# Triangular inverses of a two-block model: the joining level in 32x32 blocks, transposes on VectorE, and attention and gating taken one turn later

## What is computed

```python
lhs = eye + jnp.einsum("nbhik,nbhjk->nbhij", kb, k) * decay * (1.0 - eye)
u = solve(lhs, v * beta[..., None])
w = solve(lhs, kb * jnp.exp(gc)[..., None])
attn = jnp.einsum("nbhik,nbhjk->nbhij", q, k) * decay
...
def step(state, inp):
    v_new = u_c - jnp.einsum("bhck,bhkv->bhcv", w_c, state)
    o = jnp.einsum("bhck,bhkv->bhcv", q_c, state) + jnp.einsum("bhij,bhjv->bhiv", attn_c, v_new)
    state = state * gl[..., None, None] + jnp.einsum("bhck,bhcv->bhkv", k_c, v_new)
...
o = _rms(o) * norm_w.astype(F32) * jax.nn.silu(z...)
```

## Time and profile before

| what | value |
|---|---|
| median of 3 runs | 2035.76 us |
| lowest and highest | 2029.8 and 2036.88 us |
| the profiled execution, its own time | 2028.58 us |
| its span in the profile | 2026.8 us |
| mean granted clock of TensorE over the span, of full speed | 0.951 |
| PE / DVE / ACT / POOL busy | 1742.4 / 907.8 / 631.6 / 127.7 us |
| turns of the first loop, start to start | 128.0, 126.7 and 128.7 us |
| turns of the delta rule, start to start | 92.9 us for one, 90.9 to 91.0 us for six |

### The profile page before, as it was taken

How to read it: one execution, slowest core, us unless ns; L and a number is a source line. 1 busy time by engine, 2 the same in 40 slices (tenths; PEclk the granted TensorE clock), 3 DMA queues, 4 the chain that set the end, 5 groups by cost and what they waited for, 6 DMA issues and landing times.

```text
span 2026.8 us, 38852 instructions
## 1 busy us (share of the span) xinstructions
PE 1742.4 (86%) x16211; PEld 1135.6 (56%) x16211; DVE 907.8 (45%) x1907; ACT 631.6 (31%) x1208; POOL 127.7 (6%) x247
## 2 busy tenths in 40 slices
PE   0799999999988889999999999999699647777777
PEld 0447466574663457768686777768544523333333
DVE  5223061340621355868677686868402531111162
ACT  1133152431520153545445363545200101111112
POOL 8201000010000000000000000000000010000020
PEclk9999999999977999999999999999899669999989
DMA  8211030110821221111112111111040069999851
GB/s 321 65 43 45 0 86 2 42 45 0 305 90 52 70 66 43 43 43 44 44 42 84 44 43 43 43 43 44 15 166 11 32 253 413 407 417 397 360 176 42
DMA packets 122364, 229.15 MB, mean 113 GB/s; under 512 B 9294, under 2 KB 92587, under 8 KB 109931
## 3 DMA queue, kind: packets, MB, share of 16 engines
q1 hardware_dynamic: 100480, 194.40, 26.6%
q10 hardware_dynamic: 17996, 24.24, 3.3%
q0 software_dynamic: 3744, 8.40, 1.2%
HBM read 203.81 MB, written 28.44 MB: 115 GB/s over the span
## 4 chain that ended last, share of the span: by engine, by line
PE 45%; DVE 11%; DMA 10%; issue 1%; ACT 1%; SPq 0%; DVEq 0%; POOL 0%; ACTq 0%; POOLq 0%
PE ps L1315 11%; DMA W<-in_moe_w_up_dram 9%; PE ps L2209 6%; PE ps L1326 4%; PE ps L2517 4%; PE ps L1085 3%; PE ps L1471 3%; PE ps L2675 2%; PE ps L1449 2%; DVE W L1966 2%; PE ps L1354 1%; PE ps L1364 1%; PE ps L1374 1%; DVE W L1971 1%; DVE arena L1849 1%
## 5 line engine op out<-in xcount | busy, mean ns | idle before, releaser
L1315 PE MATMUL ps<-hT,W 128*128 128x512 f32 x512 | 230.2, 594 | 1.4 <-ACT hT L1109 1.0
L2517 PE MATMUL ps<-W,yT 128*32 128x256 f32 x2048 | 125.4, 400 | 45.4 <-DMA W<-in_moe_w_up_dram 33.9
L1315 PEld LDWEIGHTS ps<-hT,W 128*128 128x128 f32 x512 | 94.9, 190 | 98.2 <-issue 96.4
L539 PE MATMUL ps<-hT,W 128*128 128x512 f32 x288 | 137.9, 612 | 0.0
L2517 PEld LDWEIGHTS ps<-W,yT 128*32 128x32 f32 x2048 | 69.3, 115 | 106.7 <-DMA W<-in_moe_w_up_dram 41.1
L1326 PE MATMUL ps<-W,hT 128*128 128x256 f32 x512 | 117.3, 382 | 0.0
L2209 PE MATMUL ps<-W,yT 128*128 128x512 f32 x256 | 112.2, 601 | 0.9 <-ACT yT L1662 0.9
L1326 PEld LDWEIGHTS ps<-W,hT 128*128 128x128 f32 x512 | 94.8, 190 | 12.7
L1449 PE MATMUL ps<-W,arena 64*64 64x64 f32 x2560 | 89.9, 222 | 13.9 <-DVE W L1966 13.3
L1849 DVE SCALAR_TENSOR_TENSOR arena<-ps,arena 128x510 f32<-128x510 f32 (+1 forms) x128 | 95.6, 747 | 13.8 <-ACT arena L1584 10.4
L1449 PEld LDWEIGHTS ps<-W,arena 64*64 64x64 f32 x2560 | 82.6, 137 | 21.4 <-issue 20.2
(11 more groups left out here) (474 smaller groups left out, 2938.7 us busy)
## 6 DMA issues: line engine op xcount, KB each, us to landing
W<-in_moe_w_gate_dram SPq DMA_DIRECT2D x32, 1024.0 KB, 10.4
W<-in_moe_w_up_dram SPq DMA_DIRECT2D x32, 1024.0 KB, 10.7
W<-in_moe_w_down_dram SPq DMA_DIRECT2D x32, 1024.0 KB, 10.8
W<-in_w_in_dram SPq DMA_DIRECT2D x33, 512.0 KB, 6.9
W<-in_gdn_w_in_dram SPq DMA_DIRECT2D x16, 1024.0 KB, 6.9
expert_rows<-zeros ACTq DMA_DIRECT2D x1, 15360.0 KB, 56.5
W<-in_gdn_w_in_dram SPq DMA_DIRECT2D x16, 512.0 KB, 4.9
arena<-gate_rows SPq DMA_DIRECT2D x16, 512.0 KB, 6.0
```

Of the source, the lines that this page charges most:

```text
L539: mm = pe.matmul(ps[:, 5 + i % 2, :], w[:, k, j, :], hT[:, k, :], start=(k == 0), stop=(k == ND - 1))
L1315: mm = pe.matmul(ps[:, 6 + k0 % 2, :], wg[:, k, j * P:(j + 1) * P], hT[:, k, :], start=(k == 0), stop=(k == ND - 1))
L2517: mm = pe.matmul(ps[c0:c0 + m, 2 + j, 0:HID], xgT[:, b, k, c0:c0 + m], weights(j, lane)[:, k, :], start=(k == 0), stop=(k == ND - 1))
```

## The change

- **First loop, turning.** For levels 1 to 5 `flipped` and ACT's copy of the turned T are gone; DVE turns T of both heads after the masked copies (`turned`). The top level keeps `flipped`, into bank 2 for h = 0 and now bank 7 for h = 1.
- **First loop, products of the next turn.** The first 8 of the 48 products stand among the levels (`among_levels`): 2 before level 1, 1 each after levels 3 and 4, 2 after level 5, 1 inside level 6 and 1 behind it. Each chunk has 8 instead of 10. The wait for half of their weights (`sb_in`) is now ahead of level 1.
- **First loop, gate products.** PE waits for the first of the two clamped halves alone, ACT for the second.
- **Both loops, level 5.** Products are of 32x32 by 32 columns (`QUARTER`, `across`); their number is the same in the delta rule and in the first loop.
- **Delta rule, beta.** v's tokens are scaled with beta as ACT copies them: 16 copies of 128x128 (`keep_v_tokens`) at levels 2 to 4 for two of 128x512. T needs no factor: ACT places the diagonal blocks (`place_T`, four copies of 64x512, at the end of the turn), and DVE copies the level 6 blocks in four instructions.
- **Delta rule, a turn later.** `attention` of chunks 1 and 2, the two gating products, `y_columns` and the copies `keep_y` are done in the next turn (or the last stretch). SP's load of the decay rows then waits for these chunks of attention. k's tokens go to bank 4.

```diff
-        SLOT = [0, 3, 5, 8, 10]
+        SLOT = [0, 2, 4, 6, 8]
...
+            if not last:
+                pe.wait_ge(*sb_in.at("in", n))
+            among_levels(0, 2)
             for lv in range(1, LEVELS):
-                top = lv == LEVELS - 1
+                top, joined = lv == LEVELS - 1, lv == LEVELS - 2
...
-                    flipped(h, f"T {h} {lv}", HALF[0:1] if top else HALF)
+                    if top:
+                        flipped(h, f"T {h} {lv}")
...
+                if lv in (3, 4, 5):
+                    among_levels(lv - 1 if lv < 5 else 4, lv if lv < 5 else 6)
...
+            def turned(lv):
+                for h in range(2):
+                    dve.wait_ge(*rw_dve.at(f"T {h} {lv - 1}", n))
+                    dve.transpose(Tc[:, h, :, :].rearrange("p c t -> p (c t)"), TTc[:, h, :, :].rearrange("p c t -> p (c t)"))\
+                       .then_inc(*rw_dve.step(f"turned {h} {lv}"))
...
-            sp.wait_ge(*loop.dve.at(f"attention {NT - 1}", i - 1))
+            sp.wait_ge(*loop.dve.at("attention 2", i))
             gate_sums_in(i + 1)
...
+                        elif joined:
+                            for m in (0, 2, 1, 3, 4, 6, 5, 7):
+                                for to, _, of, cols in across(m):
+                                    mm = pe.matmul(small(3 * g, m)[to, cols], Nn[of, 2 * g + m // 4, m % 4, to], TTgc[of, g, m, cols], start=True, stop=True)
...
             project(s, k_, 1)
+            y_columns(s, True)
             state_update(s, 0)
...
+                    if 2 * lv + g in (5, 6, 7, 8):
+                        keep_v_tokens(s, 2 * lv + g - 5)
...
             keep_z(s, 1)
+            place_T(s)
...
             columns(s)
+            gate_ago(s)
             z_clamped(s)
             decayed_v(s, 0)
+            for c in (1, 2):
+                attention(s, c, s.ago)
             state(s, 0)
```

193 lines of the change are left out of this document (121 added, 72 removed).

## The result

The changed kernel takes **2002.08 us** (median of 4 runs, 1993.54 to 2005.47) against 2032.78 us for the kernel before (4 runs, 2028.62 to 2036.88): a ratio of 0.9843 with a 95% interval of 0.9803 to 0.9882. A later set of six runs of the changed kernel, beside eleven of before, gave 2001.79 us and 0.9857 [0.983, 0.9884]. The forecast was 1998 us, with a range of 1983 to 2016. The sum was right within 4 us, but part of that is the base: the forecast took 37.5 us off a median of 2035.76, and with its fourth run the median of before is 2032.78. The gain is 30.7 us between the medians and 26.6 between the two profiled executions, so it was over-forecast by 7 to 11 us. Several terms were off, in both directions; the rest of the document is about these.

A forecast was written before the change was run, and what follows sets the result against it. PE, busy for 86% of the span, was taken as the bound in the chunks, projections and levels. First loop 30.5 us plus delta rule 7 gave 37.5 off the 2035.76 median: 1998 us, range 1983 to 2016.

The forecast's parts named there:

- Chunks of the first loop: First loop's chunks: 8 projections fewer a turn at 0.86 us each, 6.9 us off, with no new wait.
- Levels of the first loop: Without turning on PE, a level takes 2.6 us, 3.1 with a projection; net 0.75 us earlier a turn.
- the two ahead of level 1 fit the 2.25 us idle there: First loop: two products (1.72 us) ahead of level 1 fit PE's idle time, their weights causing no wait.
- Last turn: First loop's last turn, without next-turn products: levels 4.8 us earlier, plus 0.7 from the gate products.
- rival 5: Clock falls in the last first-loop turn's levels, up to 10 us more: 2008 us; chance 0.15 together with rival 3.
- Delta rule, a turn: Delta rule turn: level 5 and returning transposes net 1.55 us, less 0.6 for ACT's copies: 1.0 us less.
- The 0.0185 of the forecast: Delta rule, level 5: us per 32x32 product, read at level 6 as 0.30 us over 16 instructions.
- Last stretch: Delta rule's end: gating, clamping and attention on DVE cost 2.1 us more, output transposes in idle PE time 1.0 less.
- Rival 4: Delta rule: decay rows land too late, ACT waits every turn, 2046 us or more; 0.05 for slower, unseen waits included.
- Rival 2: First loop: products among the levels cost full price and switching; sum about 18 us, 2018 us; chance 0.12.
- Rival 3: No delta rule gain: ACT's copies in full, 32x32 at old price; 29.5 us, 2006 us; 0.15 together with rival 5.
- Rival 1: More gain: half price for 32 columns, hidden ACT copies, no first-loop switching cost; 47.5 us, 1988 us; chance 0.18.

The follow-up runs named there:

- experiment 6: Changed kernel with none of the next turn's 48 products among the first loop's levels, each chunk having 10 again: 2017.63 us, 0.9929.
- experiment 4: Changed kernel with ACT's scaled copies of v only behind the second group's copy of V, at levels 2 to 5: 1996.84 us, 0.9822.
- experiment 5: Changed kernel with level 5 of the delta rule back at 64x64 by 64 columns in both products: 2005.91 us, 0.9871.
- experiment 8: Kernel of experiment 4 with DVE's two products for z's gate later in the delta rule's last stretch: 1992.25 us, 0.9807.

## Why the prediction was right, and where its terms were not

By the profiles of before and of the change the first loop gave 22.2 us for 30.5 forecast, the delta rule 2.7 for 7, and the stretches that should not change another 1.6. That the time came out within 4 us of 1998 owes something to luck: the median of before fell by 3 us with its fourth run, and the medians lie 4 us further apart than the profiled executions.

**Chunks of the first loop: right.** 13.2 us before, 11.48 now, no new wait, 4 x 1.72 = 6.9 us a turn.

**Levels of the first loop: handovers right, the room ahead of level 1 wrong, 1.3 us a turn.** Levels are bound by handovers, 2.72 us (2.6 forecast). With a projection they are 3.47; the forecast had 3.1 and 0.3 apart for two switches, so that price was right within 0.1. z to RU was to become 1.45 us shorter, gate products included, and became 0.13 shorter (65.32 to 65.19). The clamped half gave what it should, 0.66 for 0.7, so the levels came out 0.5 us longer instead of 0.75 shorter, and a turn gained 7.0 us in place of 8.35. The term that failed is "the two ahead of level 1 fit the 2.25 us idle there". They stand behind the same wait for DVE's masks as V of level 1, so 1.42 us of the idle time are still ahead of them (the row at 290.34, where the forecast expected 0.5), and V of level 1 starts 41.79 us after the turn's start instead of 40.72 in experiment 6, which has none there. That is 1.07 of the 1.3 us. The sum's own working has a gap there too: its pieces as listed (1.7, 0.3, less 2.6, and 0.9) add up to 0.3 us, where it says 1.55.

**A term that was not in the sum: 3.3 us for the clock.** The three turns before were 128.0, 126.7 and 128.7 us; the 1.3 and 2.0 us above the middle one are two stretches of 3.4 us at the lower clock, which the forecast left out. They are gone with the levels filled. So three turns gave 24.2 us for 25.1, 21.0 by the work and 3.3 by the clock.

**Last turn: the step that failed.** 5.5 us of gain were forecast, and 2.0 us of loss measured, in the second profile 0.5 us of gain, in experiments 4 and 5 4.6 and 3.6. The handovers do give about this gain, where nothing else happens. What the step left out is that with less work on PE, the clock falls before the levels are through (3.4 us at 532.3 and again at 545.9, then from 556.2 on), and that PE waits for "issue" (5.25 us in two places, 3.24 in the second profile, 1.71 in experiments 4 and 5, and 1.76 before). This was rival 5, with "up to 10 us, 2008": its mechanism was seen here, at a smaller price. It did not take the chunks' time, since those were at the lower clock before as well (46.2 and 45.9 us).

**Delta rule, a turn: 1.7 us gained where 1.0 was forecast.** The 32x32 products start less than 0.009 us apart, below the lower bound of 0.015 that was taken for one by its columns alone: by their starts four come 0.007 us apart and the next four 0.032 us after the first, while the profile gives each one 0.19 us, so products on different pieces of the array overlap. The 0.0185 of the forecast was a misreading: of the 16 instructions of V at level 6, ten had started by 1057.99 (the row says x10), 0.03 us each as elsewhere. V of group 1 to z is 1.64 us, bound by ACT's copy, not by PE. By experiment 5 the step is worth 1.36 us, by experiment 4 ACT's copies cost 0.7 (0.6 forecast), and the remaining 1.0 is, for the most part, the transposes (1.03) and their wait of 0.61 us for the gated output, less the 0.88 that came back at the turn's start (1.03 forecast). The rule of the Trainium skill ("TensorEngine Tiling (Array Packing)", Performance Considerations) that each matmul has about 60 cycles of overhead would have made this step worth nothing beyond the idle time; this trace disagrees, by 32 instructions in 0.27 us and by the 1.36 us a turn of experiment 5.

**Delta rule, in sum: the seven turns right by two errors, the whole 2.7 us for 7.** By experiment 5 seven turns without the lower clock and the waits for "issue" would be 617.7 us (627.3 less 9.5), 12.7 less than before; 4.6 of it were given back, which leaves 8.1, for 7 forecast. The first head, where 1 us of gain was forecast, got 2.8 slower, with 10.2 us at the lower clock in it where there were 3.4; with the first loop alone changed, and the old delta code, it is 1.5 slower already.

**Last stretch: +2.5 for +1.1.** From the first `solved` to the second it is 8.06 us for 6.26, with 3.4 us at the lower clock, and 7.67 in experiment 8 at 1.00: gating and transposes together cost 1.4 us, for 1.1 forecast, and 0.4 more by the clock. What was not seen is ACT's `place_T`, which I had costed at nothing: it is covered in the turns by the projection, and here by none. PE's first wait is now for it, 2.17 us, for 1.70 of DVE before, which is the other 0.5:

```profile
1401.85 1.29 PE L1400 MATMUL ps<-arena,W 128*128 128x128 f32 x8 [2.17 <-ACT W L1708]
1403.62 1.97 PE L1473 MATMUL ps<-ident,arena 128*128 128x128 f32 x8 [0.47 <-DVE arena L2035]
```

**The rivals.** Rival 4, decay rows late: no wait for them appears in the turns. Rival 2 is out by experiment 6: eight products cost the levels 4.5 us. Rival 3's reason is out by experiments 4 and 5 together, but its outcome came near: the delta rule alone, clock and all, is worth 0.2% (0.9981). Rival 1's half price for 32 columns was true and more, and was hidden by the clock and by ACT's two waits.

**What stays open.** Why a stretch of 3.4 us at the lower clock falls into one turn and not into another of the same code: most stand beside a wait for "issue", but four of the 20 in or behind level 5 do not, and more than ten such waits have no stretch behind them. What makes PE wait for "issue", every 256 of its instructions where it waits at all, and for how long: of the causes only the zeros were tried, and no run shifts the code by a few instructions alone. And how much of each median the two explain, since each was read in one profile of a kernel, for the changed one in two.

## What to carry to other kernels

Filling the idle time of a stretch of handovers is worth taking the work from a full stretch even when most of the fill is paid for: here 6.9 us out for 4.5 in, and the filled stretch also kept its clock. But look at what the filling waits for: it fills only the idle time behind its own place in the order. A step that makes PE quieter can lose a third of its gain to the clock and to waits for "issue", and an edit that adds instructions can lengthen code behind it. So read both per stretch in two profiles of one kernel before crediting 2 us to an edit. When an order is changed for the steady turns, go through the last, uncovered one by itself: the cheapest improvements of this study (ACT's copies behind the second group, two DVE products later in the last stretch) were there.

## What was not expected of the hardware

- 32x32 products on different pieces of the array start less than 0.009 us apart (32 in 0.27 us), where 64x64 ones start 0.03 apart.
- PE's waits for "issue" (0.3 to 3.7 us) stand at the same instructions in two executions, multiples of 256 instructions apart, and in the delta rule come up where its products are shortest: in every second turn with 32x32 products, in none with 64x64.
- The granted clock falls to 0.50 for 3.4 us in single places of a kernel that is otherwise at 1.00, at a price of 1.7 to 2.5 us each in the changed kernel's delta rule, the wait beside it included (91.70 for 89.24 us), in places that differ between two executions of one kernel.
- Twelve products more in the last turn made its chunks faster, 6.84 for 8.68 us each, with the clock at 1.00 instead of 0.50; and the whole kernel, with the copies apart, 9 us slower.
